# The spatial gate's mixing and product moved between the two value chunks of the even mixer

## The reference

```
p   = h @ w_in                                    # 1024 -> 2560
za  = gelu(p[:, :1024]);  u = za[:, :512]         # the gate's left half
vg  = layernorm(za[:, 512:])                      # the gate's right half
mixed = einsum('gts,bnsgc->bntgc', w_causal, vg) + sg_b   # 8 groups, chunks of 128 tokens
y_a = u * mixed                                   # the product
q, k = rmsnorm per head;  v = p[:, 2048:2560]     # 8 heads of 64
A[t,s] = exp(z[t,s] + suffix sums of -softplus(z))        # s < t, stick breaking
y_b = A @ v
out = concat([y_a, y_b]) @ w_out                  # 1024 -> 1024
```

## Time and profile before

| what | us |
|---|---|
| median of 3 runs | 1139.2 (1139.0 to 1139.98) |
| the profiled execution | 1136.87 |
| its span, first to last instruction | 1134.7 |
| PE busy in the span | 1103.8 (97%) |
| DVE busy | 731.2 (64%) |
| ACT busy | 516.2 (45%) |

### The profile page before, as it was taken

One profiled execution on the slowest core, in us unless ns is written; L12 is line 12 of the kernel. 1 busy time (PEld: TensorE's weight loads), 2 busy tenths in 40 slices (PEclk: granted clock), 3 DMA queues, 4 the chain that ended last, 5 costly groups with the idle time before them and its releaser, 6 DMA issues.

```text
span 1134.7 us, 21024 instructions
## 1 busy us (share of the span) xinstructions
PE 1103.8 (97%) x8656; PEld 1056.4 (93%) x8656; DVE 731.2 (64%) x790; ACT 516.2 (45%) x533; POOL 2.2 (0%) x5
## 2 busy tenths in 40 slices
PE   8999999999999999999989999999988999999998
PEld 7998887899999999989879999999878999999998
DVE  5854646668666666678746655554697886655553
ACT  5423427445544444464955443432725465343431
POOL 0000000000000000000000000000000000000000
PEclk8999999999999999999989999999988999999999
DMA  9683242345556566736324646554334344656531
GB/s 309 197 217 112 75 131 75 112 139 184 155 160 204 167 191 197 222 113 221 119 69 149 210 161 202 167 186 148 111 112 149 112 143 155 199 171 194 176 111 38
DMA packets 162589, 177.64 MB, mean 157 GB/s; under 512 B 4800, under 2 KB 148288, under 8 KB 162536
## 3 DMA queue, kind: packets, MB, share of 16 engines
q1 hardware_dynamic: 160704, 174.58, 48.6%
q10 hardware_dynamic: 1832, 2.30, 1.1%
HBM read 175.29 MB, written 1.57 MB: 156 GB/s over the span
## 4 chain that ended last, share of the span: by engine, by line
PE 80%; DVE 11%; ACT 5%; DMA 2%; issue 2%; ACTq 0%; SPq 0%; DVEq 0%
PE proj L441 49%; PE aux L849 21%; DVE wlo L1547 4%; DVE f L1550 2%; DVE f L1547 2%; ACT whi L1113 2%; PE aux L499 2%; DMA gamma_rows<-f 1%; DVE f L1553 1%; PE aux L611 1%; PE aux L600 1%; DMA f<-in_x_dram 1%; PE aux L723 1%; PE aux L708 0%; ACTq L1161 0%
## 5 line engine op out<-in xcount | busy, mean ns | idle before, releaser
L441 PE MATMUL proj<-u,whi 128*128 128x256 f32 (+1 forms) x2912 | 534.9, 285 | 4.6 <-DVE x_all L1547 2.2
L1547 DVE TENSOR_TENSOR wlo<-raw,whi 128x2048 fp32r<-128x2048 f32 (+2 forms) x179 | 374.7, 2093 | 154.3 <-ACT whi L1113 146.6
L441 PEld LDWEIGHTS proj<-u,whi 128*128 128x128 f32 x2912 | 452.9, 190 | 12.5 <-issue 8.0
L441 PE MATMUL proj<-u,wlo 128*128 128x256 f32 (+1 forms) x1456 | 412.2, 283 | 0.0
L1113 ACT ACTIVATE whi<-raw 128x2048 fp32r<-128x2048 f32 (+2 forms) x173 | 309.5, 1789 | 108.2 <-PE aux L849 40.3
L441 PEld LDWEIGHTS proj<-u,wlo 128*128 128x128 f32 x1456 | 277.4, 190 | 0.0
L849 PE MATMUL aux<-v,whi 128*128 128x256 f32 x1376 | 249.7, 283 | 1.0 <-DVE v L1547 1.0
L849 PEld LDWEIGHTS aux<-v,whi 128*128 128x128 f32 x1376 | 214.2, 192 | 1.1 <-issue 1.1
L849 PE MATMUL aux<-v,wlo 128*128 128x256 f32 x688 | 194.6, 283 | 0.0
L849 PEld LDWEIGHTS aux<-v,wlo 128*128 128x128 f32 x688 | 131.9, 192 | 0.0
L441 PE MATMUL proj<-v,whi 128*128 128x256 f32 (+1 forms) x564 | 103.8, 286 | 1.8 <-DVE v L1550 1.2
(11 more groups left out here) (277 smaller groups left out, 749.8 us busy)
## 6 DMA issues: line engine op xcount, KB each, us to landing
raw<-in_mlp_w_dram SPq DMA_DIRECT2D x64, 1024.0 KB, 5.3
raw<-in_w_in_dram SPq DMA_DIRECT2D x21, 1024.0 KB, 6.2
raw<-in_od_w_in_dram SPq DMA_DIRECT2D x12, 1024.0 KB, 5.3
raw<-in_w_ffn_gate_dram SPq DMA_DIRECT2D x22, 512.0 KB, 4.0
raw<-in_w_ffn_up_dram SPq DMA_DIRECT2D x22, 512.0 KB, 5.3
raw<-in_w_ffn_down_dram SPq DMA_DIRECT2D x21, 512.0 KB, 5.5
raw<-in_ev_w_in_dram SPq DMA_DIRECT2D x10, 1024.0 KB, 5.6
raw<-in_w_ret_out_dram SPq DMA_DIRECT2D x4, 1024.0 KB, 5.6
```

Source lines behind the costliest of these rows:

```text
L441: ins = mm(o, w_of(a, k), x_of(b, k), start=first and k == 0 and j == 0, stop=last and k == kt - 1 and j == 2, skip_group_check=skip)
L1547: return ve.tensor_tensor(o, a, b, op)
```

## The change

`mixed` becomes a turn of its own between sv0 and sv1 on PE, and DVE's product on it moves ahead of `sb_soft(2)`. The transposes `ya_turn` follow sv1 directly; the suffix sums of pairs 2 and 3 come behind them, with the values of pair 0 between the two. ACT takes the high part of the gated product ahead of the exponentials of pairs 2 and 3. DVE reads sv1 out without pumping first, so that the split of eo2 falls to the next `arrive`, that of eo0. No instruction is added or taken away.

```
-  index["sv1"]: ["mixed", "ya_turn", "yb"]
+  index["sv0"]: ["mixed"], index["sv1"]: ["ya_turn", "yb"]
...
   # PE
   project_tokens("sv0")
   sb_scores(2)
   sb_scores(3)
-  project_tokens("sv1")
   _, b = begin("mixed")
   ...                                  # 8 matmuls
-  sb_suffix(2)
-  sb_suffix(3)
+  project_tokens("sv1")
   _, b = begin("ya_turn")
   ...                                  # 8 transposes
+  sb_suffix(2)
   begin("yb")
-  for a in range(4):
+  sb_values(0)
+  sb_suffix(3)
+  for a in range(1, 4):
       sb_values(a)
...
   # ACT
   pump(index["sv1"])
-  sb_attn(2)
-  sb_attn(3)
   eng.wait_ge(sems["ya_turned"], 1)
   A.post(act(v[:, 0, 0:4, :], proj[...], ACT.Copy), "y_even_hi")
+  sb_attn(2)
+  sb_attn(3)
...
   # DVE
-  def per_token(name, dst, width=256):
-      b = arrive(name)
+  def per_token(name, dst, width=256, urgent=False):
+      b = arrive(name, urgent)
...
   value_part(0)
-  sb_soft(2)
-  sb_soft(3)
-  value_part(1)
   ...                                  # the 8 instructions of the product
+  sb_soft(2)
+  sb_soft(3)
+  value_part(1, urgent=True)
   eng.wait_ge(sems["y_even_hi"], 1)
```

More of the change, by code:

```diff
@@ L345, in build @@
         shared_turns = {index["rg0"]: ["low_norm"], index["gm3"]: ["rot"], index["uk"]: ["uk2"],
-                        index["gr0"]: ["sp0"], index["gr1"]: ["sp1"], index["gr2"]: ["sp2", "sp3"], index["sv1"]: ["mixed", "ya_turn", "yb"]}
+                        index["gr0"]: ["sp0"], index["gr1"]: ["sp1"], index["gr2"]: ["sp2", "sp3"], index["sv0"]: ["mixed"], index["sv1"]: ["ya_turn", "yb"]}
         kept_by_scalar = (index["uq0"], index["uq1"], index["uv"])
@@ L963, in _ @@
             ins.then_inc(sems["mixed"], 1)
-            sb_suffix(2)
-            sb_suffix(3)
+            project_tokens("sv1")
             _, b = begin("ya_turn")
+            vg = f("f5", 1024, 2, 512)
             read_out("mixed")
@@ L2053, in sb_soft, with value_part @@
                 B.post(stt(soft, sb_z(a), 0.0, soft, ALU.max, ALU.add), "sb_soft")
-            def value_part(c):
-                per_token(f"sv{c}", lambda j: sb_v[:, j, c * 256:(c + 1) * 256])
+            def value_part(c, urgent=False):
+                per_token(f"sv{c}", lambda j: sb_v[:, j, c * 256:(c + 1) * 256], urgent=urgent)
             sb_soft(0)
```

## The result

The changed kernel takes 1131.97 us (median of 6 runs, 1130.26 to 1133.24). The kernel before, run beside it, takes 1139.22 us (6 runs, 1136.38 to 1140.6). The ratio is 0.9943, with a 95% interval of 0.9928 to 0.9957: 7.2 us faster. The profiled execution took 1130.26 us; its span is 1128.1 us where it was 1134.7.

The account below looks back on a forecast made before the run. PE, 80% of the chain, was taken as the bound. Its work sums to 14.53 us, eo0 7.2 us earlier (4.9 wait, 2.1 slow clock, 0.2 drain): 1139.2 becomes 1132.0 us, range 1130.0 to 1134.4.

Parts of the forecast that it names:

- The binding wait: At `ya_turn`, PE waits 4.9 us for DVE's product, queued behind the split of eo2 and the sv1 read-out.
- The sum of PE's work: PE's work from the first `mixed` matmul to eo0 at full clock: 14.53 us, in place of 21.70.
- a switch of 0.15 us: On PE between the values of the head pairs and eo0, counted once: 0.15 us.
- The slow clock: PE's half clock behind the wait costs 2.1 us: 1.1 for the transposes, 1.0 for the values.
- The transposes: The eight `ya_turn` transposes on PE take 0.87 us at full clock in the new order.
- The rival at 1.94 us: The `ya_turn` transposes cost 1.94 us even in the new order: gain 1.1 us less, 1133.1 us; chance 0.05.
- The waits of the new order: From `mixed` to eo0, PE meets no wait; keeping the pump would cost 2.7 us.
- The tightest place: Values(3) on PE, wanted at 581.3, against ACT's exponential of pair 3, done at 581.1: 0.2 us of slack.
- The moved split and the loads: DVE's splits of eo2 and eo3 end at 583.6 and 588.2; they and the later loads cost PE nothing.
- What is kept behind eo0: Behind eo0 the program is unchanged and PE bound; the 7.2 us is kept, eo0 to end staying 545.4 us.
- Rival 4: Slow-clock stretches behind the change fall on PE-bound matmuls, 4.0 us each: 1140.0 or 1144.0 us; chance 0.06.
- The total: Whole kernel: median falls from 1139.2 to 1132.0 us, with profiled execution 1129.7 and median 2.3 us above it.

Follow-up runs that it names:

- e1: Kernel before with one edit: DVE reads sv1 out without pumping first, product and orders unmoved; median 1132.19 us, ratio 0.9938.
- e4: Changed kernel with the values of pair 0 behind both suffix sums, next to those of the other pairs; median 1130.58 us, ratio 0.9933.
- e5: Kernel before with 36 extra unused matmuls filling PE's 4.9 us wait; median 1135.11 us, ratio 0.9981.
- e3: Changed kernel with the pump (split of eo2) back ahead of the sv1 read-out; median 1134.86 us, ratio 0.9963.
- e6: Changed kernel with ACT's old order, exponentials of pairs 2 and 3 ahead of the product's high part; median 1133.04 us, ratio 0.9954.
- e2: Changed kernel with only `mixed` and the product moved; pump, suffix sums ahead of transposes and ACT's order as before; median 1132.77 us, ratio 0.9941.
- after: The changed kernel with all parts of the change, against the kernel before; median 1131.97 us, ratio 0.9943.
- e9: The changed kernel run once more, unaltered, against the kernel before; median 1131.39 us, ratio 0.994.
- e10: Repeat of the changed kernel with the values of pair 0 behind both suffix sums; median 1131.47 us, ratio 0.9935.
- e7: Changed kernel with the sixteen-row matmuls L900 issued three times over; median 1148.48 us (4 runs).
- e8: Changed kernel with 64 full matmuls of 128 rows ahead of the sixteen-row matmuls L900, which are issued once; median 1138.35 us (10 runs).

## Why the prediction was right, point by point

*The binding wait.* Right: the chain named the product behind a split and a read-out, and e1 shows the split to be the cause. The prediction had the product "late twice over"; the second reason, the read-out of sv1 ahead of it, cost 0.17 us of wait once the split was gone. What it did not say is that skipping the split alone suffices. Its own numbers had it: DVE was free at 572.59 + 1.95 = 574.54 and waited 2.47 us for ACT's high part ahead of the 2.30 us of the split; without both the product ends 4.77 us earlier, against a wait of 4.93. The prediction counted the gain for the whole change, and either half brings most of it.

*The sum of PE's work.* 14.53 us against 15.07 measured. The missing 0.54 us is a term mis-sized: I charged a switch of 0.15 us only ahead of eo0, but each change between the suffix sums (weights of 128 columns) and the values (64 columns) costs about as much. In the rows above, the first suffix sum to the values takes 1.83 us instead of 1.73, the values of pair 0 0.81 instead of 0.65, suffix(3) 1.93 instead of 1.73. e4 gets 0.35 of it back by having one group of values instead of two. The rest is mostly the one switch into that group (0.09) and a slower first pair (0.71 for 0.65). What in the change of form costs the time was not separated.

*The slow clock.* Predicted 2.1 us, measured 1.89 by e5. Most of the difference is again the switches: at full clock, directly ahead of values, the transposes take 1.00 us and the first pair 0.70 (e5: 584.54, 585.54, 586.24), where the sum had 0.87 and 0.65. The clock fell behind gaps of 4.93 us and 2.59 us (e3), and was at 1.00 behind gaps of 1.28 us (e6), 0.87 us (e2) and 0.70 us (e5). Behind the gap of e3 it cost 1.7 us.

*The transposes.* 0.87 us for eight at full clock, as the row of other transposes had it, in after, e4, e6, e9 and e10, where a suffix sum follows. The rival at 1.94 us is out. The Trainium skill, "TensorE: Matmul & The Clock Gate", Part 4 (PE-mode transpose), has about 275 ns for each and no fast clock for them; here eight take 0.87 us in a stretch with granted clock 1.00, so the estimate of 2.2 us from that page does not hold for a burst between other matmuls.

*The waits of the new order.* None appeared. ACT's copy came at 576.39, which is 576.93 less the 0.55 us by which this execution was ahead; the pump kept in place costs 2.59 us where 2.7 was said (e3); ACT's old order costs 1.28 us (e6). The tightest place, values(3) behind the last exponential, had 0.4 us of air (580.92 to 581.29) instead of 0.2.

*The moved split and the loads.* DVE's two splits run from 583.68 to 588.30, and the trace has no PE wait from 582 to 650 us.

*What is kept behind eo0.* From eo0 to the end 1128.1 - 582.1 = 546.0 us, against 545.4 before. In e1 to e6 it lies between 544.2 and 545.6. Rival 4 did not occur, though the slow stretches did move: between 790 and 810 us the clock was 0.75 and 0.74 in the two halves in this profile of after, where the same work before, from 797 to 817 us, had 1.00 and 0.83. The Trainium skill, "TensorE: Matmul & The Clock Gate", Part 1, says that the gate's counting doesn't restart with the kernel; that such stretches come and go between executions of equal code (e4 without and e10 with the one at L900) agrees with it.

*The total.* 1132.0 predicted, 1131.97 measured. The closeness is luck. D was off by 0.54 us, and the profiled execution by as much, 1130.26 for 1129.7. The prediction then added 2.3 us to come to the median, where the median is 1.71 above the profiled execution, and the two errors cancel. That eo0 starts at 582.09, as predicted (582.10), is luck as well: this execution came to the stretch 0.55 us earlier. Besides, medians of 6 runs of one kernel differed by 0.6 us (after and e9) and 0.9 us (e4 and e10).

## What to carry to other kernels

When an engine works in program order, look for bulk work with a far deadline (here the split of eo2, done at 579.3 and wanted at 589.27 + 2 x 5.76 = 600.8) ahead of a short operation that the bounding engine waits for. Move that first, alone, and measure: a reordering of three engines did no more here than one skipped call (15.07 against 15.06 us of D; with the tail of e4 it would have been 14.72). Look at the clock behind an idle gap of the matmul engine: gaps of 2.6 and 4.9 us cost a further 1.7 to 1.9 us of slow clock here, gaps of up to 1.3 us left it at 1.00. Compare variants by the distance between two instructions in their traces, which repeats to 0.01 us where whole runs spread over 2 us and more.

## What the runs showed of the hardware

The matmul engine's clock can fall from 1.00 to 0.50 with the engine 100% busy (7.00 of 7.00 us in e1's window above). From matmuls on whose weights fill only 16 partitions, the way from L893 to L913 was 18.96 us or up to 3.1 us longer in ten profiles of kernels that are equal up to there: five undisturbed (before, after, e3, e4, e9), four at 22.0 to 22.1 (e1, e2, e6, e10) and one at 20.5 (e5). Three times as many such matmuls brought a stretch of 14 us at 0.52 (e7); with full ones instead the one profile stayed at 1.00 (e8). The Trainium skill, "TensorE: Matmul & The Clock Gate", Part 1, describes the gate as following how busy the engine is; in the sense in which this profile counts busy, that did not hold. What it is in these matmuls, the few rows or their plain float32 form (the trace has two instructions for each), was not separated; but from 574.50 to 582.09 us PE in after runs nothing but transposes and matmuls of that form on all 128 rows, at 1.00. Part of the spread of this kernel's times comes from here: it is decided before the changed stretch begins.
